# A layer norm behind the output projection, split around its last chunk

## The reference

```
x = layer_norm(ALPHA * x + mix @ w_out, ln1_w, ln1_b)     # mean, variance over 1024, eps 1e-5
scores = sigmoid(x @ router_w);  sel = scores + router_bias
# the best of 4 groups by the sum of its top 2 of sel; top 2 experts of that group;
# gates = scores of the two / their sum
ff = sum over experts e of gates[:, e] * ((silu(x @ w_gate[e]) * (x @ w_up[e])) @ w_down[e])
x = layer_norm(ALPHA * x + ff, ln2_w, ln2_b)
```

## Time and profile before

| | us |
|---|---|
| median of three runs | 939.57 (936.17 to 939.82) |
| the profiled execution | 938.43 |
| its span, first to last instruction | 936.6 |
| TensorE busy | 898.0 (96%) |
| VectorE, ScalarE, GpSimd busy | 373.1, 279.2, 103.5 |
| mean granted TensorE clock | 0.991 |

### The profile page before, as it was taken

One profiled execution on the slowest core, in us unless ns is written; L12 is line 12 of the kernel. 1 busy time (PEld: TensorE's weight loads), 2 busy tenths in 40 slices (PEclk: granted clock), 3 DMA queues, 4 the chain that ended last, 5 costly groups with the idle time before them and its releaser, 6 DMA issues.

```text
span 936.6 us, 15754 instructions
## 1 busy us (share of the span) xinstructions
PE 898.0 (96%) x6507; PEld 558.4 (60%) x6507; DVE 373.1 (40%) x963; ACT 279.2 (30%) x595; POOL 103.5 (11%) x166
## 2 busy tenths in 40 slices
PE   9999999898998999999999999999998999999986
PEld 6878777776886444444425786777875343434424
DVE  1368776966314311121313335666336020201314
ACT  3534543231204220101003248888304120101003
POOL 2232030635000000000000101111400000000000
PEclk9999999999999999999999999999999999999998
DMA  9963254893997699999996884545797999999991
GB/s 377 356 247 141 103 192 169 338 386 142 412 423 322 243 420 417 420 421 421 421 420 277 334 341 143 185 153 212 268 420 303 402 422 417 421 420 421 420 398 58
DMA packets 41308, 299.84 MB, mean 320 GB/s; under 512 B 5064, under 2 KB 6600, under 8 KB 12808
## 3 DMA queue, kind: packets, MB, share of 16 engines
q1 hardware_dynamic: 36000, 268.52, 70.9%
q0 software_dynamic: 4544, 29.65, 8.5%
q10 hardware_dynamic: 688, 0.60, 0.2%
HBM read 283.32 MB, written 15.53 MB: 319 GB/s over the span
## 4 chain that ended last, share of the span: by engine, by line
PE 76%; DMA 11%; DVE 8%; ACT 2%; issue 2%; POOL 1%; ACTq 0%; DVEq 0%; POOLq 0%
PE bank L1330 19%; PE bank L1354 10%; PE bank L1526 8%; PE bank L962 7%; PE bank L1209 6%; DMA ring<-in_w_down 6%; PE bank L1513 5%; PE bank L1396 3%; PE bank L1309 3%; PE bank L1230 3%; PE bank L1368 1%; DMA W<-in_conv_cols 1%; DVE ring L2243 1%; DMA spread<-xd_rows 1%; DMA spread<-v_rows 1%
## 5 line engine op out<-in xcount | busy, mean ns | idle before, releaser
L1330 PE MATMUL bank<-ring,W 128*32 128x512 f32 x1280 | 201.8, 593 | 3.0 <-DMA ring<-in_w_up 1.5
L962 PE MATMUL bank<-xT,ring 128*128 128x264 f32 x704 | 165.0, 390 | 1.7 <-DMA ring<-in_w_ab 1.1
L962 PEld LDWEIGHTS bank<-xT,ring 128*128 128x128 f32 x704 | 131.9, 191 | 32.3 <-issue 9.1
L1330 PE MATMUL bank<-A,W 128*32 128x512 f32 x624 | 140.1, 593 | 0.0
L1330 PEld LDWEIGHTS bank<-ring,W 128*32 128x32 f32 x1280 | 55.7, 110 | 101.7 <-issue 96.3
L1354 PE MATMUL bank<-ring,W 128*32 128x512 f32 x528 | 77.1, 593 | 2.8 <-DMA ring<-in_w_down 2.8
L2516 DVE TENSOR_TENSOR gkg<-gkg,bank 128x512 f32<-128x512 f32 x16 | 11.0, 688 | 171.4 <-PE bank L1330 171.4
L1526 PE MATMUL bank<-xT,ring 128*128 128x264 f32 x320 | 78.0, 391 | 0.0
L1526 PEld LDWEIGHTS bank<-xT,ring 128*128 128x128 f32 x320 | 58.3, 190 | 11.1 <-issue 1.6
L1354 PE MATMUL bank<-A,W 128*32 128x512 f32 x288 | 62.7, 593 | 0.0
L1330 PEld LDWEIGHTS bank<-A,W 128*32 128x32 f32 x624 | 36.8, 110 | 36.8 <-issue 36.6
(11 more groups left out here) (345 smaller groups left out, 1250.0 us busy)
## 6 DMA issues: line engine op xcount, KB each, us to landing
ring<-in_w_gate SPq DMA_DIRECT2D x40, 1024.0 KB, 15.8
ring<-in_w_up SPq DMA_DIRECT2D x39, 1024.0 KB, 18.3
ring<-in_w_down SPq DMA_DIRECT2D x33, 1024.0 KB, 20.0
ring<-in_w_ab SPq DMA_DIRECT2D x10, 2048.0 KB, 8.9
A<-in_w_up SPq DMA_DIRECT2D x20, 1024.0 KB, 19.5
A<-in_w_gate SPq DMA_DIRECT2D x18, 1024.0 KB, 17.6
ring<-in_w_c SPq DMA_DIRECT2D x8, 2048.0 KB, 11.3
A<-in_w_down SPq DMA_DIRECT2D x13, 1024.0 KB, 12.2
```

Source lines behind the costliest of these rows:

```text
L962: mm = pe.matmul(ab_bank(m)[:, 0:T], slot(AB_IN0 + m // 4, 8)[:, c, (m % 4) * P:(m % 4 + 1) * P], xT[:, c, :], start=(c == 0), stop=(c == ...
L1330: mm = pe.matmul(out[ROWS * g:ROWS * (g + 1), :], xg[:, c, E_G * b + g, :], w[g][:, c % 4, :], start=(c == 0), stop=(c == DC - 1))
```

## The change

Norms 0 and 2 are computed in another order.

- After chunks 0 and 1, TensorE multiplies their sum with `mean_ones` (`shift_sum`); VectorE takes four times that, the mean that these two chunks alone would give, as a `shift` and adds its negative to all chunks. Chunks 4 to 7 get the shift while their products are made, the others in between. A small product takes the same shift out of the folded router weights.
- Squares and router products of the chunks 0 to 6, the mean product of `presum` and the product of the router's bias are issued ahead of the last output chunk (`squares_of`, `before_last`). `behind_last` issues the mean, squares and router products of chunk 7.
- VectorE's `variance` takes the square of the rest mean (`delta`) off the mean of the squares. Ln and Exp follow from that.
- The eight subtractions of the mean before the squares are gone. The rest mean enters the token copies as a bias (`row_shifts`), one more step stands in the decode inputs, and `xT` loses it in one operation ahead of `norm_scale`.
- The bias product for all tokens is made once, so the logits take three small products instead of six. They lie in bank 7; the token transposes lie in banks 4, 5, 6 and 1.
- The transposes of tokens 0 and 1 come ahead of the roots. `keep_clock` issues three products of 128x512 ahead of the counting products and one behind them, into a bank that nobody reads.
- Counters of semaphores change to match.

```diff
...
+        CENTERED = (0, 1, 4, 2, 5, 3, 6, 7)
...
-            return bank[2 if k % 2 else 6]
+            return bank[2 if k % 2 else 1]
...
-            return bank[0 if k % 2 else 7]
+            return bank[0]
...
+            return bank[(4, 5, 6, 1)[i]]
...
+        row_shifts = area(10610, 2)
+        folded_sum = area(10692, ROUTER_W)
+        shift = area(8320, T)
+        delta = area(8584, T)
...
+            def shift_sum(layer):
+                pe.wait_ge(sem("norm_ahead"), 5 * layer + 1)
+                pe.matmul(bank[6][:, 0:T], mean_ones[:, :], presum[:, :], start=True, stop=True)
+                pe.matmul(bank[7][:, 0:ROUTER_W], mean_ones[:, :], folded_sum[:, :], start=True, stop=True).then_inc(
+                    sem("norm_sum"), 1)
+            def squares_of(layer, *chunk_list):
+                for c in chunk_list:
+                    i = CENTERED.index(c)
+                    pe.wait_ge(sem("norm_squares"), SQUARES * layer + i + 1)
+                    mm = pe.matmul(square_bank(2 * layer)[:, 0:T], ones[:, :], lnsq[:, c, :], start=(i == 0), stop=(i == DC - 1))
+                if i == DC - 1:
+                    mm.then_inc(sem("norm_sum"), 1)
+            def logits_of(c):
+                q = c % 4
+                return pe.matmul(bank[2][32 * q:32 * q + 32, 0:T], folded[:, c, :], xT[:, c, :], start=(c < 4), stop=(c >= 4))
+            def before_last(layer):
+                pe.wait_ge(sem("norm_ahead"), 5 * layer + 2)
+                pe.matmul(mean_bank(2 * layer)[:, 0:T], mean_ones[:, :], presum[:, :], start=True, stop=False)
+                for c in range(DC - 1):
+                    logits_of(c)
+                pe.matmul(bank[7][:, 0:3 * E_N].rearrange("p (b e) -> p b e", b=3), ones[:, :],
+                          folded_bias[:, 0:E_N].rearrange("p (o e) -> p o e", o=1).to_broadcast([P, 3, E_N]), start=True, stop=False)
+            def behind_last(layer):
+                pe.wait_ge(sem("norm_centered"), DC * layer + DC)
+                pe.matmul(mean_bank(2 * layer)[:, 0:T], mean_ones[:, :], xT[:, DC - 1, :], start=False, stop=True
                           ).then_inc(sem("norm_sum"), 1)
...
+                squares_of(layer, DC - 1)
+                logits_of(DC - 1).then_inc(sem("moe_logits"), 1)
...
+                def turn_tokens(i):
+                    b, c0 = i // 2, 4 * (i % 2)
+                    for c in range(c0, c0 + 4):
+                        tr = pe.transpose(token_bank(i)[:, (c % 4) * P:(c % 4 + 1) * P],
+                                          xT[:, c, b * P:(b + 1) * P], ident[:, :])
+                    tr.then_inc(sem("xtm_turned"), 1)
+                def keep_clock(count):
+                    w = expert_half(layer, 0, 0, 0, 0)
+                    for i in range(count):
+                        pe.matmul(bank[0][:, :], ident[:, :], w[:, i, :], start=True, stop=True)
+                turn_tokens(0)
+                turn_tokens(1)
+                pe.wait_ge(sem("norm_variance"), layer + 1)
+                for b in range(2):
+                    pe.transpose(bank[3][:, 3 * P * b:3 * P * b + P], delta[:, b * P:(b + 1) * P], ident[:, :])
                 pe.wait_ge(sem("norm_roots"), 2 * layer + 1)
                 for b in range(2):
                     tr = pe.transpose(bank[3][:, P * (b + 1):P * (b + 2)], lnr[:, b * P:(b + 1) * P], ident[:, :])
                 tr.then_inc(sem("xtm_turned"), 1)
-                def turn_tokens(i):
...
-                turn_tokens(0)
                 pe.wait_ge(sem("moe_logits"), 3 * layer + 2)
-                for b, n in enumerate((P, P, NB)):
-                    pe.matmul(bank[2][0:n, 288 + 16 * b:304 + 16 * b], logits4[:, b * P:b * P + n], quarter[:, :],
-                              start=True, stop=False)
-                    mm = pe.matmul(bank[2][0:n, 288 + 16 * b:304 + 16 * b], ones[:, 0:n], folded_bias[:, 0:E_N],
-                                   start=False, stop=True)
+                for b, n in ((2, NB), (0, P), (1, P)):
+                    mm = pe.matmul(bank[7][0:n, 16 * b:16 * b + 16], logits4[:, b * P:b * P + n], quarter[:, :],
+                                   start=False, stop=(b == 1))
                 mm.then_inc(sem("moe_logits"), 1)
-                for i in range(1, 4):
-                    turn_tokens(i)
+                turn_tokens(2)
+                turn_tokens(3)
+                expert_ready(pe, layer, 0, 0, 0)
+                keep_clock(3)
                 stage_wait(pe, 3 * layer + 3)
                 pe.wait_ge(sem("moe_chosen"), layer + 1)
                 chosen = rt[:, 3, :, :]
                 pe.matmul(bank[3][:, 0:2 * E_N], strict[:, :], chosen[:, 0:2, :], start=True, stop=True).then_inc(
                     sem("moe_places"), 1)
-                pe.matmul(bank[1][:, 0:2 * E_N], ones[:, :], chosen[:, 0:2, :], start=True, stop=True).then_inc(
+                pe.matmul(bank[7][:, 0:2 * E_N], ones[:, :], chosen[:, 0:2, :], start=True, stop=True).then_inc(
                     sem("moe_places"), 1)
+                keep_clock(1)
...
                 out_part(m, ssd_half)
-            for m in range(4, DC):
+            shift_sum(0)
+            for m in range(4, DC - 1):
                 out_part(m, gla_half + ssd_half)
-            residual_sum(0)
-            norm_squares(0)
+                if m == 5:
+                    squares_of(0, 0, 1)
+            squares_of(0, 4, 2, 5, 3, 6)
+            before_last(0)
+            out_part(DC - 1, gla_half + ssd_half)
+            behind_last(0)
...
+                if k % 2 == 0:
+                    act.wait_ge(sem("norm_variance"), k // 2 + 1)
+                    st.run(act.activation(lnr[:, :], lnr[:, :], ACT.Ln, bias=eps_col[:, :]))
...
-                    act.activation(xtm[:, i // 2, (i % 2) * 512:(i % 2 + 1) * 512], bank[4 + i][:, :], ACT.Copy,
-                                   scale=row_roots[:, i // 2:i // 2 + 1]).then_inc(sem("xtm_copied"), 1)
+                    act.activation(xtm[:, i // 2, (i % 2) * 512:(i % 2 + 1) * 512], token_bank(i)[:, :], ACT.Identity,
+                                   scale=row_roots[:, i // 2:i // 2 + 1], bias=row_shifts[:, i // 2:i // 2 + 1]).then_inc(sem("xtm_copied"), 1)
...
+                def centered(ins):
+                    ins.then_inc(sem("norm_centered"), 1)
+                def shifted_ahead(m):
+                    st.add(dve.scalar_tensor_tensor(xT[:, m, :], xT[:, m, :], ALPHA, shift, ALU.mult, ALU.add))
+                def center(c):
+                    centered(dve.tensor_tensor(xT[:, c, :], xT[:, c, :], shift, ALU.add))
+                def add(m):
+                    st.settle()
+                    out_ready(m)
+                    centered(dve.tensor_tensor(xT[:, m, :], xT[:, m, :], out_bank(m)[:, 0:T], ALU.add))
+                def sum_up(a, c, n):
+                    dve.wait_ge(sem("norm_centered"), DC * layer + n)
+                    st.run(dve.tensor_tensor(presum, a, xT[:, c, :], ALU.add))
+                for m in range(4):
+                    out_ready(m)
+                    st.add(dve.scalar_tensor_tensor(xT[:, m, :], xT[:, m, :], ALPHA, out_bank(m)[:, 0:T], ALU.mult, ALU.add))
                     if m == 1:
+                        st.settle()
                         st.run(dve.tensor_tensor(presum, xT[:, 0, :], xT[:, 1, :], ALU.add))
-                    if 2 <= m < DC - 1:
-                        st.run(dve.tensor_tensor(presum, presum, xT[:, m, :], ALU.add))
-                    if m == DC - 2:
                         dve.sem_inc(sem("norm_ahead"), 1)
...
-            def layer_norm(k, src):
-                if k % 2 == 0:
-                    dve.wait_ge(sem("norm_sum"), 2 * k + 1)
...
+                st.add(dve.tensor_tensor(folded, folded, bank[7][:, 0:ROUTER_W].rearrange("p (o e) -> p o e", o=1).to_broadcast(
+                    [P, DC, ROUTER_W]), ALU.subtract))
+                st.settle()
+                shifted_ahead(4)
+                center(0)
+                center(1)
+                add(4)
+                shifted_ahead(5)
+                center(2)
+                sum_up(xT[:, 0, :], 1, 2)
+                sum_up(presum, 4, 3)
+                add(5)
+                shifted_ahead(6)
+                center(3)
+                sum_up(presum, 2, 4)
+                sum_up(presum, 5, 5)
+                add(6)
+                shifted_ahead(7)
+                sum_up(presum, 3, 6)
+                sum_up(presum, 6, 7)
+                dve.sem_inc(sem("norm_ahead"), 1)
+                add(7)
+            def variance(layer):
+                mean = mean_bank(2 * layer)[:, 0:T]
+                dve.wait_ge(sem("norm_sum"), 5 * layer + 2)
+                st.run(dve.tensor_copy(delta, mean))
+                st.run(dve.scalar_tensor_tensor(lnr[:, :], mean, -1.0, delta, ALU.mult, ALU.mult))
+                dve.wait_ge(sem("norm_sum"), 5 * layer + 3)
```

(23 more changed lines are left out.)

99 lines of the change are left out of this document (35 added, 64 removed).

## The result

The changed kernel takes 941.24 us (median of 20 runs, 938.62 to 942.60), the kernel before, run beside it, 938.87 us (20 runs, 935.17 to 941.65). The ratio is 1.0024 [1.0013, 1.0035]: **slower by 2.3 us, with an interval of 1.2 to 3.3 us.** It is within half a per cent, the bound that the prediction took for no change, but it is a real loss, where the forecast said +0.4.

A forecast was written before the change was run, and what follows sets the result against it. Weight stream and products hang on the first gate product's start. Layer one: 5.34 - 3.58 + 0.10 - 1.82 = +0.04; layer two +0.34; together +0.4 us on 938.43, 938.8, stated as 939.4; range 934.5 to 944.5.

The forecast's parts named there:

- One event per layer: Start of each layer's first gate product: weight stream and products hang on it, each microsecond ahead counting one for one.
- Part 1: Work moved or added ahead of the last output product: delays it in full, 5.34 us per layer, bounds 4.9 to 5.7.
- Two rounds of four at 0.445: Seven router products ahead of the last output product, priced four abreast at the stream's rate: 0.89 us.
- The full 1.10 of the row: Router products priced at the profile's duration for eight, four abreast, to their last end: 1.10 us, used in the upper bound.
- The shift pair: Product for the shift and small product for the folded router sums, ahead of the last output product: 0.445 and 0.22 us.
- Part 2: Relay from last add to routing gets shorter: 5.76 us against 9.34, 3.58 saved per layer, bounds 3.0 and 4.2.
- VectorE's steps hold the barrier: Stage barrier behind VectorE's decode inputs holds ScalarE's sigmoid to 5.43 us after the last add, though TensorE would allow 4.85.
- Part 3: Filler products before the gather keep the clock up: 1.82 and 1.72 us gained by layer; the last filler costs 0.1.
- Part 4: Behind the routing: VectorE's subtraction of the rest mean from `xT`, 2.4 us, and the later fills stay hidden, costing nothing.
- (a): Rival: fillers themselves run at half clock and hold up the counting products; +4.8 us per layer, 948.9; 11%.
- (b): Rival: the clock still falls in the gather despite the fillers; +3.5 us, 942.9; 14%.
- (c): Rival: several terms too high (small products, barrier, last filler, layer two's wait); -1.1 and -1.3 us per layer, 937.0; 28%.

The follow-up runs named there:

- e1: The kernel before with fillers alone: two 128x512 products behind the token transposes, one behind the counting products; ratio 0.9959 to the kernel before.
- e2: The changed kernel without its four fillers per layer; ratio 1.0052 to the kernel before.
- e3: The changed kernel with seven chunks' router products and the bias product behind the last chunk, one filler fewer; ratio 0.9976 to the kernel before.
- e4: e3 with the presum product and the squares of chunk 6 behind the last chunk too; ratio 0.9963 to the kernel before.
- e6: e5 with the second layer's shift sum two products later, inside chunk 4; ratio 0.9968 to the kernel before.
- e5: e4 with VectorE's four decode-input steps moved from ahead of the stage barrier to behind the first one-hot; ratio 0.9975 to the kernel before.
- e7: e1 without the filler behind the counting products, two fillers left; ratio 0.9967 to the kernel before.
- e10: e6 with no fillers at all, the new norm order alone; ratio 0.9987 to the kernel before.
- e8: The changed kernel once more, unchanged, on another chip; ratio 1.0028 to the kernel before.

## Why the prediction was wrong

The forecast had the right mechanism and the wrong sizes. The time is inside its range, but the change costs 2.1 us by the distances where the sum had 0.4, because all the terms that were off by more than 0.02 erred one way.

- **One event per layer: right.** From layer one's first gate product to the last weights' use at the end of its experts it is 187.40 us before (307.48 to 494.88), 187.26 after, and 187.19 to 187.34 in e1, e2 and e3. In layer two it is 218.8 to 219.1 from the first gate product to the end of the span in eleven profiles, and 220.8 in e1, which has its dip of the clock there. Stream and products move together.
- **Part 1, the step that failed most: 5.75 / 6.17 us instead of 5.34 / 5.54.** The squares and the product of `presum` cost 0.445 each, as said (e4: 0.89 for two). The seven router products with the bias cost 1.45 (what e3 gives back), against 0.89 + 0.22. "Two rounds of four at 0.445" takes the products at their rate and leaves out what it costs to enter and leave them. TensorE's loader idles at both places (0.34 us <-issue before L1266, 0.42 before L1274, the first two rows of the timeline above), and the records of the products, which follow each other by 0.22 us in the stream around them, start 0.32 apart into the router products and 0.33 apart out of them. That is 0.1 us lost at each. The bias product takes another 0.33 where I had 0.22. At both places the weight tile changes between 128 columns and 32, and the products between one at a time and four abreast; no run separates the two. The chain has 1.02 for the fourteen and 0.35 for the bias. The full 1.10 of the row, which I kept as the upper bound, was the better reading. The 25 ns of the Trainium skill (TensorE: Matmul & The Clock Gate, Back-to-back issue gap) for a small product is further from these rows than the 0.22 that I took. The shift pair costs 0.74 (e4's 3.41 less six squares of 0.445) against 0.67. In layer two the shift sum waits another 0.42 (e6), not 0.20. Its timeline:

```profile
684.86 0.43 DVE L2392 TENSOR_TENSOR W<-xT 128x264 f32<-128x264 f32 x1
685.40 0.30 PEld L1250 LDWEIGHTS bank<-W,mean_ones 128*128 128x128 f32 x2 [0.57 <-DVEq L2393]
685.40 0.71 PE L1250 MATMUL bank<-W,mean_ones 128*128 128x264 f32 x2 [0.15 <-DVEq L2393]
```

- The sum of two chunks is done at 685.29 and the product starts at 685.40: VectorE first waits for its own result and then signals in an instruction of its own. I had counted the sum and not these 0.11 us. The other 0.10 is in the product: with its weights loaded only now it takes 0.71 us to its end, where the same kind of product in the stream takes 0.61 (283.12, L1271). In e6 both are gone.
- **Part 2: 3.43 saved, not 3.58.** The roots (3.60 against 3.58) and the logits (3.63 against 3.62) are as predicted. Then VectorE's copy of the turned roots (L2449) starts 0.50 us after the logits, since the transposes (L1317) start only with the roots and the copy needs them; in the kernel before, where the logits started later than these transposes, it stood 0.35 behind (296.01). The rest of the chain stands 0.15 later with it: sigmoid at 5.58 instead of 5.43, routing at 5.91 instead of 5.76. That VectorE's steps hold the barrier was right (0.68 <-DVEq L304; e5 removes it). What the prediction never asked is whether the work moved ahead had cost anything where it was. With the subtractions of the mean gone it would not have: e3 and e4 move 2.3 us of it back and the relay grows by 0.03.
- **Part 3: 1.52 / 1.41 gained, not 1.72 / 1.62.** The fillers end before the choice (TensorE idles 0.64 us before L1331), the clock holds, the gather is right in kind: 3.65 us, where I took 3.56. The fourth filler pushes the gather by 0.18 and shortens it by 0.11; it costs 0.08 net (e1 against e7), the 0.10 of the prediction, and was not needed. The counting products start 0.03 later.
- **Part 4: right.** The subtraction takes 2.35 us (L2472) and hides, and the next fill goes out 3.70 us after the first gate product, as before (311.18 less 307.48).
- **The step that failed, in one sentence.** The sum priced entering and leaving the router products, the small bias product and VectorE's signal at nothing or at the pitch of a stream, so part 1 came to 5.34 / 5.54 us where 5.75 / 6.17 were measured; the relay (0.15) and the gather with its last filler and its start (0.20) add the rest of the 0.76 and 1.00 us per layer.
- **Rivals.** (a) fell, the fillers ran at full clock (three products in 2.74 us, L1308). (b) fell, both gathers ran at 1.00. (c), that terms were on the high side, fell the other way: of its four, the small products did not hide, the barrier did bind, the last filler cost what was said, and layer two waited 0.42.

## What to carry to other kernels

Before work is moved ahead of a wait, ask what it costs where it stands: behind the last output chunk TensorE had idle time under VectorE's and ScalarE's steps, and ahead of it none, so moving the router products, the bias, `presum` and the last square was a loss of 2.3 us per layer. Judge such a change by the distance between two events around it, in each layer, and not by times or spans of single profiles. And be careful with a sum of hand-overs never seen: here their errors all had one sign, and the full duration of the nearest row was closer than the rate (1.02 us measured for the router products, 1.10 in the row, 0.89 by the rate).

## What the runs showed of the hardware that I had not expected

- Two products of dead data (1.9 us, e7) in an idle stretch of TensorE are worth 1.63 and 1.53 us in the two layers, because the next 16 small products (32 records) run at 2.4 GHz in place of 1.2. In e10 the clock fell after idle stretches of 1.70 and 0.59 us with sixteen transposes right before them; in e7 it held after 0.32 and 0.59 us behind two fillers.
- Going from products of 128 weight columns to four abreast of 32, and back, shows as 0.34 and 0.42 us of idle loader and delays the next product by 0.1 us each time.
- A wait of 1.34 us for a transfer is followed by a dip of the clock in some executions and not in others of the same kernel (the changed kernel and e8), 1.70 us each time. The Trainium skill (TensorE: Matmul & The Clock Gate, The HAM clock gate) says that the monitor runs freely and so the point of a change varies; a dip that comes and goes agrees with that, while the fall in the gather came in every profile without fillers (before, e2, e10), in both layers.
